# Weight-block sums of the recurrent heads: made by accumulating transfers from GpSimd in place of VectorE

## The reference, cut to what matters

```python
h = _rmsnorm(x, norm_w)                               # x: 512 tokens x 1024
proj = jnp.einsum('bsd,de->bse', h, w_in)             # ten groups of 1024 columns
(q_raw, ffwd_raw, fbwd_raw, i_raw, ga_raw,
 u_raw, v_raw, gb_raw, ma_raw, mb_raw) = jnp.split(proj, split_points, axis=-1)
y_a = _hgrn2_branch(q_raw, ffwd_raw, fbwd_raw, i_raw, ga_raw, ...)   # 8 recurrent heads
y_b = _spatial_gating_branch(u_raw, v_raw, gb_raw, ...)
...
# then a merge, attention, memory attention and a mixture of experts
```

## Time and profile before

| | us |
|---|---|
| median of 3 runs | 1466.37 (1465.72 to 1466.39) |
| the profiled execution | 1469.64 |
| its span, first to last instruction | 1467.8 |

### The profile page before, as it was taken

The page is one execution under the profiler, slowest core; times in us unless marked ns, Lnnn a source line. Parts: engine busy times, 40 slices in busy tenths (PEclk is TensorE's granted clock), DMA queues, the critical chain, the costliest instruction groups (busy, mean ns, idle before and its releaser), DMA issues. The chain is left out here.

```text
span 1467.8 us, 15643 instructions
## 1 busy us (share of the span) xinstructions
PE 1388.6 (95%) x5584; PEld 829.2 (56%) x5584; DVE 872.6 (59%) x1919; ACT 430.9 (29%) x710; POOL 99.0 (7%) x146
## 2 busy tenths in 40 slices
PE   7999999999999999999999899998899898999876
PEld 3455555666666768888888444445485435333322
DVE  5467687898898957867566448835374414222211
ACT  2434444354444315101012233134313421000000
POOL 0000000000000000000000025300000000222221
PEclk9999999999999999999999999999999999999999
DMA  7031021121110224213233233102031757999997
GB/s 296 29 115 58 29 58 29 47 84 58 58 58 1 72 100 173 86 58 115 86 144 115 87 114 86 44 9 86 29 115 71 301 185 289 403 406 406 410 408 281
DMA packets 41389, 205.45 MB, mean 140 GB/s; under 512 B 7840, under 2 KB 9504, under 8 KB 34528
## 3 DMA queue, kind: packets, MB, share of 16 engines
q1 hardware_dynamic: 34016, 189.74, 34.6%
q0 software_dynamic: 4608, 8.40, 2.4%
q10 hardware_dynamic: 2688, 6.29, 1.1%
HBM read 196.67 MB, written 12.58 MB: 143 GB/s over the span
## 5 line engine op out<-in xcount | busy, mean ns | idle before, releaser
L565 PE MATMUL gla_proj<-hT,weight_slots 128*128 128x512 f32 x672 | 295.1, 592 | 1.9 <-DVE hT L1035 1.9
L565 PEld LDWEIGHTS gla_proj<-hT,weight_slots 128*128 128x128 f32 x672 | 125.1, 190 | 147.7 <-issue 146.9
L3356 PE MATMUL moe_banks<-weight_slots,moe_room 128*64 128x512 f32 x400 | 92.5, 612 | 10.2 <-DMA weight_slots<-in_w_gu 7.5
L2101 PE MATMUL mid_p_proj<-hT,weight_slots 128*128 128x512 f32 x208 | 92.1, 595 | 1.8 <-PEq L187 1.8
L3513 DVE SCALAR_TENSOR_TENSOR moe_room<-moe_banks,moe_kept,moe_room 128x256 f32<-128x256 f32 x16 | 7.7, 483 | 128.8 <-ACT moe_room L3468 128.8
L734 ACT ACTIVATE gla_level_decay<-gla_level_decay 128x1024 f32<-128x1024 f32 x56 | 59.0, 1054 | 49.4 <-DVE gla_level_decay L922 48.9
L2101 PEld LDWEIGHTS mid_p_proj<-hT,weight_slots 128*128 128x128 f32 x208 | 39.0, 190 | 51.7 <-issue 51.6
L3356 PEld LDWEIGHTS moe_banks<-weight_slots,moe_room 128*64 128x64 f32 x400 | 29.6, 140 | 64.9 <-issue 54.2
L2285 POOL TENSOR_TENSOR qkT_bias<-y,mid_head_cos 128x512 f32<-128x512 f32 x4 | 5.6, 1394 | 856.2 <-ACT y L2160 856.2
L692 ACT COPY gla_raw<-gla_proj 128x512 f32<-128x512 f32 x38 | 22.4, 590 | 137.5 <-PE gla_proj L565 137.5
L593 PEld LDWEIGHTS gla_level<-gla_level_q,gla_level_k 128*128 128x128 f32 x448 | 55.0, 192 | 8.3 <-issue 6.7
(11 more groups left out here) (525 smaller groups left out, 2664.5 us busy)
## 6 DMA issues: line engine op xcount, KB each, us to landing
weight_slots<-in_w_gu SPq DMA_DIRECT2D x25, 2048.0 KB, 22.6
weight_slots<-in_w_gla SPq DMA_DIRECT2D x40, 512.0 KB, 3.6
weight_slots<-in_w_dn SPq DMA_DIRECT2D x10, 2048.0 KB, 33.0
weight_slots<-in_w_merge SPq DMA_DIRECT2D x32, 512.0 KB, 4.7
weight_slots<-in_w_out SPq DMA_DIRECT2D x16, 512.0 KB, 4.4
weight_slots<-in_w_v SPq DMA_DIRECT2D x3, 2048.0 KB, 8.2
hT<-in_w_gu SPq DMA_DIRECT2D x3, 2048.0 KB, 39.3
weight_slots<-in_w_u SPq DMA_DIRECT2D x8, 512.0 KB, 4.6
```

Source lines behind the costliest of these rows:

```text
L565: last = nc.tensor.matmul(pj[:, n % 2, :], lhsT, rhs, start=(k == 0), stop=(k == KT - 1))
L2101: last = nc.tensor.matmul(pw[:, n % 2, :], a, b, start=(k == 0), stop=(k == KT - 1))
L3356: last = nc.tensor.matmul(pG[rows, e, :], hgT[:, k, rows], core.as_gate_up(at[k // 4])[:, x, k % 4, :], start=(k == 0), stop=(k == KT - 1))
```

## The change

The four DVE sums of a pair go. GpSimd issues ten transfers per pair, each of 256 KB: one adds the high half of the second tile, read from HBM, onto b12; three copy the low half of the first tile from HBM into `sums[1]`, `sums[0]` and `sums[2]`, each after the product of the pair before that read it; six add further halves onto the three sums, each after the transfer before it on that sum has landed. `sums[2]` is now plus (`sums[1]` + b21), so the token forms 1 and 2 and four of DVE's combinations change sign. PE waits on the new semaphores.

```diff
+        self.sum_in = [ctx.enter_context(nc.semaphore(f"weight_sum_{n}")) for n in range(3)]
+        self.both_in = ctx.enter_context(nc.semaphore("second_tile_summed"))
...
-                pe.wait_ge(summed, 4 * n + 2)
+                pe.wait_ge(sum_in[1], 48 * (n + 1))
...
-                pe.wait_ge(summed, 4 * n + 3)
+                pe.wait_ge(both_in, 16 * (n + 1))
...
+                pe.wait_ge(sum_in[0], 32 * (n + 1))
...
-                pe.wait_ge(summed, 4 * n + 4)
+                pe.wait_ge(sum_in[2], 64 * (n + 1))
...
-            def weight_sums(dve, n):
-                for slot, times in zip(PAIR_SLOTS[n], PAIR_LOADS[n]):
-                    dve.wait_ge(core.w_in[slot], w0[slot] + 16 * times)
-                if n:
-                    dve.wait_ge(y1_done, n)
-                    dve.wait_ge(z3_done, n)
-                nc.vector.tensor_tensor(sums[:, 0], b11(n), b12(n), ALU.add).then_inc(summed, 1)
-                dve.wait_ge(summed, 4 * n + 1)
-                nc.vector.tensor_tensor(sums[:, 1], sums[:, 0], b22(n), ALU.add).then_inc(summed, 1)
-                nc.vector.tensor_tensor(b12(n), b12(n), b22(n), ALU.add).then_inc(summed, 1)
-                dve.wait_ge(summed, 4 * n + 2)
-                nc.vector.scalar_tensor_tensor(out=sums[:, 2], in0=sums[:, 1], scalar=-1.0, in1=b21(n),
-                                               op0=ALU.mult, op1=ALU.subtract).then_inc(summed, 1)
+            def add(out, a, b):
+                return nc.vector.tensor_tensor(out, a, b, ALU.add)
...
+                if n == 1:
+                    sub(forms[:, 1], forms[:, 0], hT[:, 0:H, 0:Q]).then_inc(formed, 1)
+                if n == 2:
+                    nc.vector.scalar_tensor_tensor(out=forms[:, 2], in0=forms[:, 1], scalar=-1.0, in1=hT[:, H:KT, Q:T],
+                                                   op0=ALU.mult, op1=ALU.subtract).then_inc(formed, 1)
...
-                sub(part(n, 0, 1), part(n, 1, 0), pZ[:, 0:Q]).then_inc(u2_out, 1)
+                add(part(n, 0, 1), part(n, 1, 0), pZ[:, 0:Q]).then_inc(u2_out, 1)
...
-                        weight_sums(dve, 5)
...
-                    if n == -1 and l == 4:
-                        weight_sums(dve, 0)
...
+            @block.gpsimd
+            def _(pool):
+                def weight_sums(n):
+                    (kind, m), (kind2, m2) = PAIRED[n]
+                    first, second = dram["w_" + kind][m], dram["w_" + kind2][m2]
+                    low, high = slice(0, H * P), slice(H * P, 2 * H * P)
+                    pool.wait_ge(core.w_in[PAIR_SLOTS[n][1]], w0[PAIR_SLOTS[n][1]] + 16 * PAIR_LOADS[n][1])
+                    pool.dma_start(b12(n), second[:, high], accum_op=ALU.add).then_inc(both_in, 16)
+                    for k, free in ((1, z1_done), (0, y1_done), (2, z3_done)):
+                        if n:
+                            pool.wait_ge(free, n)
+                        pool.dma_start(sums[:, k], first[:, low]).then_inc(sum_in[k], 16)
+                    for step, (k, src) in enumerate(((1, second[:, low]), (0, second[:, low]), (2, second[:, low]),
+                                                     (1, second[:, high]), (2, second[:, high]), (2, first[:, high]))):
+                        pool.wait_ge(sum_in[k], 16 * (n * (k + 2) + (1, 1, 1, 2, 2, 3)[step]))
+                        pool.dma_start(sums[:, k], src, accum_op=ALU.add).then_inc(sum_in[k], 16)
+
+                for n in range(len(PAIRED)):
+                    weight_sums(n)
...
-                    if i >= FIRST_PAIRED:
-                        weight_sums(dve, i - FIRST_PAIRED + 1)
```

More of the change, by code:

```diff
@@ L442, in gla_stage @@
             "x1_out", "u2_out", "u3_out", "c22_out", "c21_out", "c12_out"))
-        summed, formed = core.sem("weights_summed"), core.sem("h_formed")
+        sum_in, both_in = core.sum_in, core.both_in
+        formed = core.sem("h_formed")
         w0 = list(core.w_n)
@@ L864, in form @@
                 dve.wait_ge(formed, min(n, 2))
-                a, b = ((hT[:, 0:H, 0:Q], forms[:, 0]), (hT[:, H:KT, Q:T], forms[:, 1]), (hT[:, H:KT, 0:Q], forms[:, 1]))[n - 1]
-                sub(forms[:, n], a, b).then_inc(formed, 1)
+                if n == 1:
[3 more added lines that the diff above has]
+                                                   op0=ALU.mult, op1=ALU.subtract).then_inc(formed, 1)
+                if n == 3:
+                    add(forms[:, 3], hT[:, H:KT, 0:Q], forms[:, 1]).then_inc(formed, 1)
             def second(dve, n):
@@ L870, in second @@
                 dve.wait_ge(z1_done, n + 1)
-                sub(part(n, 0, 1), part(n, 1, 0), pZ[:, 0:Q]).then_inc(u2_out, 1)
+                add(part(n, 0, 1), part(n, 1, 0), pZ[:, 0:Q]).then_inc(u2_out, 1)
             def third(dve, n):
                 dve.wait_ge(z2_done, n + 1)
-                sub(part(n, 1, 1), part(n, 1, 0), pZ[:, 0:Q]).then_inc(u3_out, 1)
+                add(part(n, 1, 1), part(n, 1, 0), pZ[:, 0:Q]).then_inc(u3_out, 1)
             def rest_22(dve, n):
@@ L883, in rest_21 @@
                 dve.wait_ge(z3_done, n + 1)
-                sub(part(n, 1, 0), part(n, 1, 0), pZ[:, 0:Q]).then_inc(c21_out, 1)
+                add(part(n, 1, 0), part(n, 1, 0), pZ[:, 0:Q]).then_inc(c21_out, 1)
             def rest_12(dve, n):
```

## The result

| | median us | runs |
|---|---|---|
| before | 1467.14 | 6 |
| changed | 1480.29 (1478.31 to 1486.65) | 6 |

The ratio is 1.0093, with an interval of 1.0077 to 1.0108: the change makes the kernel slower by 0.8 to 1.1%. Forecast were 1470.0 us and a high end of 1474.5: the sign was right, the size far too small. The profiled execution took 1486.65 us (span 1484.8), the longest of the six; a second one is among the experiments.

The account below looks back on a forecast made before the run. PE's own work, busy 95% of the span, was taken to set the pace. Pair 5's 3.0 us lateness less 0.9 gain, plus 1.5 for the clock, gave 1466.4 + 3.6 = 1470.0 us, range 1465.5 to 1474.5.

Parts of the forecast that it names:

- What is removed, the gain of 0.9 us: At pair 5, DVE without its sums finishes its last combination at most 0.9 us earlier, shortening PE's 1.87 us wait.
- Pairs 1 to 4: In pairs 1 to 4, sum 1 lands near 317 us, 21 us before z1 reads it; no cost.
- Pair 5, 3.0 us late: Pair 5's copies wait for pair 4's products, so z1 starts at 512.45 instead of 509.46, 3.0 us late.
- one of the prediction's own signs of being wrong: Additions landing in under 3.6 us or over 7 us would show the forecast wrong.
- Prices: GpSimd transfers: copy 1.07 us issue, 3.6 to land; addition 1.35 and 4.45, between gather and scatter (1.61, 5.3).
- The clock, 1.5 us: After PE idles 3.0 us at pair 5, TensorE's granted clock falls for a while, costing 1.5 us more.
- Rival (1): Pair 5's last addition on sum 1 lands in time; 1465.5 to 1468 us, in the middle 1466.9; chance 0.36.
- Rival (2): GpSimd can't write descriptors beside busy DVE, so z1 of pair 5 is 10 us late; 1477 us; chance 0.06.
- Rival (3): Transfers cost full-queue prices, 15.0 us a copy, 11.7 an addition; pairs 1 to 5 late; 1504 us; chance 0.04.
- Rival (4): DVE's relief reaches further, bringing back nearly all PE's waits for DVE in these heads; 1463 us; chance 0.04.
- The sum: For the whole kernel, the end moves 2.1 us and the clock adds 1.5 us, 3.6 us slower in all.

Follow-up runs that it names:

- the runs without late sums: Two runs against the kernel before: the same 60 transfers reordered so sum 1 goes first, 1467.16 us; no sums made by any engine, 1465.16 us.
- plain copies: Changed kernel with its 42 accumulating transfers made plain, writing over what they should add to; 1472.46 us, 1.0020 to 1.0051 against the kernel before.
- SP's loads late: Changed kernel with pair 4's sums back on VectorE and SyncE's two 512 KB loads waiting for z1 of pair 5; 1473.37 us.
- the other order: Changed kernel with the same 60 transfers ordered by need, sum 1's copy and additions first; 1467.16 us, 0.9975 to 1.0013 against the kernel before.
- pair 4 on DVE: Changed kernel with only pair 4's sums made by VectorE again, pair 5's left to GpSimd; 1474.29 us, 1.0018 to 1.0050 against the kernel before.
- The runs with one late pair each: Changed kernel with one pair's sums back on VectorE: pair 5's, leaving pair 4 late, 1476.24 us; pair 4's, leaving pair 5 late, 1474.29 us.
- the second profile of the changed kernel: Changed kernel unaltered, run and profiled again beside the kernel with extra matmuls; median 1481.24 us, 1.0082 to 1.0126 against the kernel before.

## Why the prediction was wrong, point by point

- **What is removed, the gain of 0.9 us: right.** The wait of 1.87 us fell to 0.94; the runs without late sums gain 0.8 us.
- **Pairs 1 to 4, "21 us early … No cost": this step failed.** It holds for pairs 1 to 3. For pair 4 the slack of pair 1 was carried over, though pair 4 opens at the very start of the last head: its loads go out at 477.64 and its z1 starts at 492.78. The prediction's own prices say so: sum 1 was to land 13.5 us after the loads (303.5 to 317), and 482 + 13.5 = 495.5 is later than 492.78. With prices kept and the slack read at pair 4, it would have been 2.7 us late in the sum, not 21 early. The measured lateness is 5.3 to 8.1 us: three copies side by side took 5.5 to 6.7 us to land, not 3.6, and in the first profile the last addition took 6.1, not 4.45. Pair 4 alone costs the last head 7.5 us.
- **Pair 5, 3.0 us late: the mechanism was right, one term too small.** The third copy behind z3 (502.28, forecast 501.73) and the last addition on sum 1 (507.80, forecast 507.25) came as worked out. That addition landed in 7.5 us in place of 4.45: the contention with SyncE's two loads was 2.7 us, not 0.6. Without them it took 4.8 us, and the wait was 2.67 us. A landing over 7 us was one of the prediction's own signs of being wrong.
- **Prices: issue below both bounds, landing between them and beyond.** Issue was 0.86 us in the median, under 1.07 and 1.61. Additions landed in 3.6 us at best, as the gather, in 5.3 in the median, as the scatter at its best, and in 8.8 at most in the changed kernel. The Trainium skill, page "DMA: Bandwidth & Descriptors", section "Anatomy of one DMA — SWDGE (gpsimd) path", gave an estimated 2.6 us for a weight block. Plain transfers come near it at best (2.6 us in the run with plain copies, 4.5 in the median), additions never do: no trace here has a landing of one under 3.6 us.
- **The clock, 1.5 us: right in kind, small in size.** In the changed kernel each wait cost some 1.8 to 2.5 us, and there were two. Near the 3.0 us of waiting that the prediction reckoned with it came out both ways: z1 lost 0.1 us after 2.67 us (SP's loads late) and 1.6 us after 2.80 us (plain copies).
- **Rival (1)**, in time: it did not come; only the other order has no wait. **Rival (2)**, GpSimd held up until DVE stops: refuted for the instructions that DVE runs here. With pair 4 on DVE, GpSimd issued five transfers from 502.28 to 507.80, and in the stretch below (columns of the earlier trace rows) three of them beside a DVE that was busy 4.00 of 4.00 us. **Rival (3)**, full queues: in the changed kernel copies landed in 9.3 us at most and additions in 8.8, none in 11.7 or 15. Its sum was also too small by its own prices: sum 1's copy, issued after z1 at about 494.8, would have landed at 509.8 and the two additions at some 533, not 526.2. **Rival (4)**: the relief is not seen to reach further.

```profile
504.00:508.00 4.00, 3.10 (x27) 2.79 (x26) 4.00 (x13) 1.80 (x3) 1.90 (x3) 1.00 0.89 206
```

- **The sum.** Forecast 2.1 + 1.5 = 3.6 us. The runs with one late pair each show 7.5 (pair 4) + 6.6 (pair 5) = 14.1, and the second profile of the changed kernel 14.3; 7.5 belong to the pair that the prediction dismissed in two words. That the change came out slower, as forecast, owes as much to pair 4 as to the wait that was forecast.

## What to carry to other kernels

A slack belongs to one place: where a loop's last iterations are arranged in another way, read the issue of the load and the first reader there, and not in an iteration that stands for the others. In a queue that keeps its order, a transfer that waits for a load holds up everything behind it, so each transfer stands where its reader comes, and transfers with sources of their own go ahead of it. Price a transfer by what runs beside it, above all by loads that start at about the same time.

## What the runs showed of the hardware

- An accumulating transfer of 256 KB issued by GpSimd takes an estimated 144 packets where a plain one takes 80 (7488 with 42 of 60 adding, 4800 with none; the 18 copies reckoned at 80 in both). It keeps the DMA engines busy an estimated 2.0 times as long (from 15.2 against 8.9% for the same 15.73 MB), and costs 0.86 us to issue against 0.54.
- An idle time of PE alone doesn't tell whether the clock falls. After 2.67 us (SP's loads late) z1 took 1.96 us, and the granted clock was 1.00 from 512 to 518 us. After 2.80 and 2.31 us (plain copies) z1 took the times of the two rows below, nearly twice 1.89, and the granted clock was 0.59 in 496 to 500 and 0.57 in 517 to 521. Even the idle time of 2.10 us before the next stage came out both ways: 0.50 right behind it with SP's loads late (560 to 562), 1.00 with pair 4 on DVE (562 to 572). What makes the difference was not tried.

```profile
496.44 3.51 PE L509 MATMUL gla_pair<-weight_slots,gla_w_sums 128*128 128x256 f32 x8 [2.80 <-issue]
...
517.36 3.55 PE L509 MATMUL gla_pair<-weight_slots,gla_w_sums 128*128 128x256 f32 x8 [2.31 <-issue]
```
